# Adaptive-weight units moved from two expert layers' value stages to three feed-forward layers, and gate groups spread over the late expert units

## The reference

```python
def peer_ffn(h, w_q, sub_keys, u, v):          # first block, both layers
    q = (xc @ w_q); s = einsum(q, sub_keys)    # scores against 2 x 128 keys per head
    ... top 16 of each half, top 16 of the 256 sums -> eid, g = softmax(cv)
    a = gelu(einsum('td,thkd->thk', xc, u[eid]))
    return einsum('thk,thkd->td', g * a, v[eid])

def second_block(...):
    c_act = silu(c)
    for l in range(2):
        mod = c_act @ ada_w[l] + ada_b[l]      # 9 vectors
        h = rmsnorm(x, ...) * (1 + sc1) + sh1; y = swiglu(h, ...)        # ffn
        x = x + 0.5 * g1 * rmsnorm(y, ...)
        h = ...; y = hybrid_mixer(h, ...)                                # attention
        h = ...; y = swiglu(h, ...)                                      # ffn
```

## Time and profile before

| | |
|---|---|
| median of 3 runs | 3534.74 us |
| runs | 3529.9 to 3535.18 us |
| profiled execution | 3530.44 us |
| its span (first to last instruction) | 3528.7 us |
| TensorE busy | 3265.3 us, 93% of the span |
| VectorE busy | 2171.8 us, 62% |
| ScalarE busy | 1543.9 us, 44% |
| GpSimd busy | 469.3 us, 13% |
| mean granted TensorE clock | 0.950 |
| moved by DMA | 632.32 MB, mean 179 GB/s |

### The profile page before, as it was taken

How to read it: one execution, slowest core, us unless ns; L and a number is a source line. 1 busy time by engine, 2 the same in 40 slices (tenths; PEclk the granted TensorE clock), 3 DMA queues, 4 the chain that set the end, 5 groups by cost and what they waited for, 6 DMA issues and landing times.

```text
span 3528.7 us, 60815 instructions
## 1 busy us (share of the span) xinstructions
PE 3265.3 (93%) x20336; PEld 2856.0 (81%) x20336; DVE 2171.8 (62%) x4110; ACT 1543.9 (44%) x2941; POOL 469.3 (13%) x563
## 2 busy tenths in 40 slices
PE   6999999899998889999999999989896998988898
PEld 4779999877776745789998777779875998986798
DVE  6538878778884144288787788865433545534354
ACT  2123478744442133234788444454322444433343
POOL 0120035611110000100356111100000000000000
PEclk9999999999999766999999999999998999999899
DMA  7664544389994300345443898855431553543354
GB/s 277 219 203 157 172 156 136 115 322 317 313 313 144 107 30 18 131 159 172 158 136 109 312 317 311 312 182 184 148 133 60 184 183 127 184 134 104 102 184 143
DMA packets 176451, 632.32 MB, mean 179 GB/s; under 512 B 23608, under 2 KB 23616, under 8 KB 175328
## 3 DMA queue, kind: packets, MB, share of 16 engines
q1 hardware_dynamic: 134416, 491.48, 40.9%
q0 software_dynamic: 41920, 139.60, 11.4%
q10 hardware_dynamic: 16, 0.01, 0.0%
HBM read 627.74 MB, written 9.50 MB: 181 GB/s over the span
## 4 chain that ended last, share of the span: by engine, by line
PE 86%; DVE 7%; ACT 2%; DVEq 2%; issue 1%; POOL 1%; DMA 1%; ACTq 0%; SPq 0%; POOLq 0%
PE ps L531 20%; PE ps L411 15%; PE ps L421 10%; PE ps L423 10%; PE ps L422 10%; PE ps L519 2%; PE ps L517 2%; PE ps L518 2%; PE ps L433 2%; PE ps L464 2%; PE ps L442 2%; PE ps L788 1%; PE ps L789 1%; PE ps L494 1%; DVE unit_low L1203 1%
## 5 line engine op out<-in xcount | busy, mean ns | idle before, releaser
L1203 DVE TENSOR_TENSOR unit_low<-ring,unit_high 128x1024 fp32r<-128x1024 f32 x744 | 948.6, 1275 | 446.9 <-ACT unit_high L868 436.4
L868 ACT CAST unit_high<-ring 128x1024 fp32r<-128x1024 f32 x744 | 778.1, 1046 | 678.6 <-PE ps L423 522.6
L421 PE MATMUL ps<-expert_x_high,unit_high 128*128 128x256 f32 x1792 | 517.1, 289 | 17.6 <-DVE unit_low L1203 17.4
L422 PE MATMUL ps<-expert_x_low,unit_high 128*128 128x256 f32 x1792 | 505.0, 282 | 0.0
L423 PE MATMUL ps<-expert_x_high,unit_low 128*128 128x256 f32 x1792 | 503.6, 281 | 0.0
L411 PE MATMUL ps<-hT,ring 128*128 128x256 f32 (+1 forms) x1776 | 414.6, 393 | 49.9 <-ACT hT L903 27.2
L411 PEld LDWEIGHTS ps<-hT,ring 128*128 128x128 f32 (+1 forms) x1776 | 341.7, 195 | 114.6 <-issue 49.2
L421 PE MATMUL ps<-norm_parts,unit_high 128*128 128x256 f32 x1408 | 403.2, 286 | 27.4 <-DVE norm_parts L1208 27.4
L423 PE MATMUL ps<-norm_parts,unit_low 128*128 128x256 f32 x1408 | 401.5, 285 | 0.0
L422 PE MATMUL ps<-norm_parts,unit_high 128*128 128x256 f32 x1408 | 400.5, 284 | 0.0
L421 PEld LDWEIGHTS ps<-expert_x_high,unit_high 128*128 128x128 f32 x1792 | 342.6, 191 | 25.6 <-DVE unit_low L1203 12.4
(11 more groups left out here) (219 smaller groups left out, 5210.1 us busy)
## 6 DMA issues: line engine op xcount, KB each, us to landing
ring<-stream SPq DMA_DIRECT2D x914, 512.0 KB, 3.3
score<-ada POOLq DMA_DIRECT2D x224, 512.0 KB, 5.2
arena<-bias_tiles POOLq DMA_DIRECT2D x48, 192.0 KB, 2.7
arena<-ada SPq DMA_DIRECT2D x8, 1024.0 KB, 17.2
bias_tiles<-bias_rows POOLq DMA_DIRECT2D x8, 768.0 KB, 16.7
x_home<-x POOLq DMA_DIRECT2D x2, 1024.0 KB, 4.1
hT<-cond POOLq DMA_DIRECT2D x2, 1024.0 KB, 6.0
x<-x_home POOLq DMA_DIRECT2D x2, 1024.0 KB, 7.9
```

The lines of the kernel that those rows point to most:

```text
L421: pe.matmul(out, hi[:, kt, :], xh[:, kt, :], start=(kt == 0), stop=False)
L422: pe.matmul(out, hi[:, kt, :], xl[:, kt, :], start=False, stop=False)
L868: nc.scalar.copy(hi, ring[:, unit % SLOTS, :]).then_inc(whi_ready, 1)
L1203: V.tensor_tensor(out=lo, in0=ring[:, unit % SLOTS, :], in1=hi, op=ALU.subtract).then_inc(wlo_ready, 1)
```

## The change

- In each value stage 48 adaptive units are computed instead of 96, in two of five units from unit 10 on; the code is written out, without a loop. `cond_late` holds one condition row of 1024 instead of two.
- The other 96 are computed in ffn0, ffn1 and ffn2, 32 in each: one with each of 16 of the 22 pairs and one with each of 16 of the down units. They have slots and a condition row of their own in `arena` (`ada_ffn`, `cond_ffn`); GpSimd issues their transfers, ScalarE the silu at the start of ffn0. VectorE's loops there are written out.
- The late expert units are handled as 2 x 28 with 32 gate groups in each 28: the units 6, 13, 20 and 27 of each 28 carry two groups, the others one. TensorE loops twice over 28 units, ScalarE and VectorE are written out.

```diff
-SINGLE = 48
+LOOP_UNITS = 28
+LOOP_GATES = 32
+ADA_FFN = EARLY + 96
+        def gates_after(e):
+            return range(LOOP_GATES * e // LOOP_UNITS, LOOP_GATES * (e + 1) // LOOP_UNITS)
...
-                with pe.Fori(0, SINGLE // 4) as i:
-                    for e in range(4):
-                        expert(DIRECT + BEFORE + e, i, 4)
-                        gate(e, i, 4)
-                for e in range(NE - DIRECT - BEFORE - SINGLE):
-                    expert(DIRECT + BEFORE + SINGLE + e)
-                    gate(SINGLE + 2 * e)
-                    gate(SINGLE + 2 * e + 1)
+                with pe.Fori(0, 2) as i:
+                    for e in range(LOOP_UNITS):
+                        expert(DIRECT + BEFORE + e, i, LOOP_UNITS)
+                        for g in gates_after(e):
+                            gate(g, i, LOOP_GATES)
...
             def ffn(ph, no, u):                      # ScalarE
+                if no == 0:
+                    act.wait_ge(c_late_in, 16 * 3)
+                    nc.scalar.activation(cond_ffn, cond_ffn, ACT.Silu).then_inc(c_ready, 1)
...
+            def ada_next(n, cond_row):               # VectorE
+                v, k = n // KD, n % KD
+                ada_unit(v % 3, k, n, cond_row)
+                if k == KD - 1:
+                    ada_take(v, v % 3)
...
+                for f in range(NF):                  # feed-forward, pairs
...
+                    V.tensor_tensor(out=hparts[:, 1, f, :], in0=hid[:, e, :], in1=hparts[:, 0, f, :],
+                                    op=ALU.subtract).then_inc(hlo_ready, 1)
+                    if no < 3 and 4 <= f < 20:
+                        if no == 0 and f == 4:
+                            dve.wait_ge(c_ready, 4)
+                        ada_next(m, cond_ffn)
+                        m += 1
+                for f in range(NF - 2):              # down units
+                    low(u + f + 2, n + f + 2)
+                    if no < 3 and f < 16:
+                        ada_next(m, cond_ffn)
+                        m += 1
...
+                def weigh_loop(it, last):
+                    for e in range(LOOP_UNITS):
+                        for g in gates_after(e):
+                            weigh(g, it, LOOP_GATES)
+                            if g == gates_after(e)[0]:
+                                low(u + DIRECT + BEFORE + e + 2, n + DIRECT + BEFORE + e + 2, it, LOOP_UNITS)
+                            if not last or g + 2 < LOOP_GATES:
+                                columns_hot(g + 2, it, LOOP_GATES)
                         dve.drain()
-                        unit_times(DIRECT + BEFORE + e, i, 4)
+                        unit_times(DIRECT + BEFORE + e, it, LOOP_UNITS)
                         dve.drain()
...
-                        if 6 <= e < 30 if late else e % 4 < 3:      # in turn(), 96 in a stage
+                for e in range(NE):
+                    if e + 2 < NE:
+                        activations_low(e + 2, a + e + 2)
+                        low(u + e + 2, n + e + 2)
+                    if e >= 8 and e % 5 in (0, 2):
+                        if m == EARLY + 48 * l:
+                            dve.wait_ge(c_ready, 2 + l)
+                        ada_next(m, cond_late)
+                        m += 1
...
-                pool.dma_start(cond_late, cond.to_broadcast([P, 2 * D])).then_inc(c_late_in, 16)
+                pool.dma_start(cond_late, cond[0:1, l * D:(l + 1) * D].to_broadcast([P, D])).then_inc(c_late_in, 16)
...
+            def ffn(ph, no):                         # GpSimd
+                if no == 0:
+                    pool.wait_ge(x_ready, KD * phases.index(ph))
+                    pool.dma_start(cond_ffn, cond[0:1, D:2 * D].to_broadcast([P, D])).then_inc(c_late_in, 16)
+                m = ADA_FFN + 32 * no
+                for q in range(m, m + 32):
+                    if q >= ADA_FFN + SLOTS:
+                        pool.wait_ge(ada_used, q - SLOTS + 1)
+                    pool.dma_start(ada_ffn[:, q % SLOTS], ada[q]).then_inc(ada_late[q % SLOTS], 16)
```

More of the change, by code:

```diff
@@ L1114, in rows_hot @@
                     for t in range(4):
-                        nc.scalar.activation(hot[:, g % 2, 2, t, :], iota, ACT.Square, bias=oT4[:, 0, it + g // 4, g % 4, t:t + 1])
+                        nc.scalar.activation(hot[:, g % 2, 2, t, :], iota, ACT.Square, bias=oT4[:, 0, it * (per // GB) + g // GB, g % GB, t:t + 1])
                     act.drain()
@@ L1133, in peer, with rows_loop @@
                         rows_hot(1)
-                with act.Fori(0, SINGLE // 4) as i:
-                    for e in range(4):
-                        gelu_aside(DIRECT + BEFORE + e, i, 4)
-                        rows_hot(e + 2, i, 4)
-                for e in range(NE - DIRECT - BEFORE - SINGLE):
-                    gelu_aside(DIRECT + BEFORE + SINGLE + e)
-                    for g in range(SINGLE + 2 * e + 2, min(SINGLE + 2 * e + 4, S // 4)):
-                        rows_hot(g)
+                def rows_loop(it, last):
+                    for e in range(LOOP_UNITS):
+                        gelu_aside(DIRECT + BEFORE + e, it, LOOP_UNITS)
+                        for g in gates_after(e):
+                            if not last or g + 2 < LOOP_GATES:
+                                rows_hot(g + 2, it, LOOP_GATES)
+                rows_loop(0, False)
+                rows_loop(1, True)
                 u += NE
@@ L1307, in take_outputs, with ada_unit @@
                 V.tensor_copy(oT[HD:P, chunk, :], ps[bank + 1][HD:P, 0:S]).then_inc(o_read, 1)
-            def ada_unit(c, k, n, cond_row, it=0, per=0):
+            def ada_unit(c, k, n, cond_row):
                 if n < FIRST:
@@ L1669, in peer @@
                 dve.drain()
-                with dve.Fori(0, SINGLE // 4) as i:
-                    for e in range(4):
-                        weigh(e, i, 4)
-                        low(u + DIRECT + BEFORE + e + 2, n + DIRECT + BEFORE + e + 2, i, 4)
-                        columns_hot(e + 2, i, 4)
+                def weigh_loop(it, last):
+                    for e in range(LOOP_UNITS):
+                        for g in gates_after(e):
+                            weigh(g, it, LOOP_GATES)
+                            if g == gates_after(e)[0]:
+                                low(u + DIRECT + BEFORE + e + 2, n + DIRECT + BEFORE + e + 2, it, LOOP_UNITS)
+                            if not last or g + 2 < LOOP_GATES:
+                                columns_hot(g + 2, it, LOOP_GATES)
                         dve.drain()
-                        unit_times(DIRECT + BEFORE + e, i, 4)
+                        unit_times(DIRECT + BEFORE + e, it, LOOP_UNITS)
                         dve.drain()
-                for e in range(NE - DIRECT - BEFORE - SINGLE):
-                    for g in range(SINGLE + 2 * e, SINGLE + 2 * e + 2):
-                        weigh(g)
-                        if g + 2 < S // 4:
-                            columns_hot(g + 2)
-                        if g % 2 == 0:
-                            low(u + DIRECT + BEFORE + SINGLE + e + 2, n + DIRECT + BEFORE + SINGLE + e + 2)
-                    dve.drain()
-                    unit_times(DIRECT + BEFORE + SINGLE + e)
-                    dve.drain()
+                weigh_loop(0, False)
+                weigh_loop(1, True)
                 u += NE
@@ L1696, in activations_low @@
                                     op=ALU.subtract).then_inc(alo_ready, 1)
[L1698 to L1714 removed]
                 for k in range(2):
                     activations_low(k, a + k)
[L1718 to L1725 removed]
+                m = EARLY + 48 * l
+                for e in range(NE):
[7 more added lines that the diff above has]
+                        m += 1
+                assert m == EARLY + 48 * (l + 1)
                 wait_used(dve, u + NE - 1)
@@ L1878, in _ @@
                     hyb(ph, int(ph[-1]))
+                elif ph != "ffn3":
+                    ffn(ph, int(ph[-1]))
 def vec_of(ph):
```

82 lines of the change are left out of this document (25 added, 57 removed).

## The result

| | us, median | runs | profiled execution | its span |
|---|---|---|---|---|
| before (same chip) | 3532.59 | 8 | 3530.44 (run ahead of the change) | 3528.7 |
| changed | 3559.99 | 8 (3546.1 to 3571.98) | 3557.78 | 3555.3 |

Ratio 1.0077, 95% interval 1.0056 to 1.0098: 27 us slower. The forecast was 3545.5 with a range of 3518 to 3568, so the direction and the range held, and the size was short by 14 (as a difference: +10.8 forecast, +27.4 measured). Beside this the changed kernel scatters by 26 us between executions, the kernel before by 8.

What follows compares the result with a forecast made beforehand. The chain of waits, 86% of it TensorE's, was taken as the bound. Terms -1.3 - 2.3 + 0.5 + 6.4 + 7.5 = +10.8 gave 3541 for the profiled execution, 3545.5 as a median; range 3518 to 3568.

Steps and rivals of the forecast that it cites:

- part 3: Late expert units: spreading the gate groups makes each double wait 2.3, +3.2 a stage, +6.4 for both, clock apart.
- Part 1: Value stages: 48 adaptive units fewer in each save nothing themselves; shorter silu -1.3, hardware loop gone -2.3.
- the steady state: Value stages: units hang on TensorE, ScalarE's cast and VectorE's low part, so removing adaptive units gains 0.
- -1.3: Start of both value stages: the shorter silu removes TensorE's idle of 0.64 behind it, twice; bounds 0 and -2.6.
- -2.3: Second value stage: removing VectorE's hardware loop takes its length from 379.9 towards the first's 377.6; bounds 0 and -2.3.
- a rule that would have given up to 81 a stage: Value stages: queues share 16 DMA engines, so 48 transfers fewer could save up to 81 us; forecast took 0.
- Part 2: ffn0 to ffn2: 96 adaptive units fit VectorE's gaps under ScalarE's cast; +0.5 for all three layers, bounds 0 and +14.
- adaptive units lengthen the layers: Feed-forward layers: only 0.2 of room in each gap, +14 on top, 3559; chance 0.06.
- 1.6 that is always there, and 0.7 by which VectorE has fallen behind: First double of the late expert units: the two pieces of TensorE's forecast wait of 2.3 for its second gate.
- 5 x 0.16: Later doubles: VectorE falls behind 0.16 a unit after each double, raising their wait from 1.6 up to 2.4.
- the third rival: Late expert units: VectorE's unit drops to 3.7 or less, waits 1.6, no clock fall; -8, 3527; chance 0.22.
- TensorE's clock: Doubles of the late expert units: three falls to half clock at 2.5 each among 16 waits, +7.5.

Runs made afterwards that it cites:

- ada_moved_alone: Changed kernel with the gate groups put back behind single units and the last eight doubled, so only the adaptive units are moved: 3549.95 us, ratio 1.0055.
- no_late_units: Changed kernel without any adaptive unit's transfer or product in the value stages and feed-forward layers: 3547.4 us, ratio 1.0049.
- gates_spread_alone: Kernel before with only the gate groups spread; adaptive units stay in the value stages: 3551.7 us, ratio 1.0063.
- columns_first: Changed kernel with VectorE's column one-hots issued ahead of the weight low part in every late unit: 3534.4 us, ratio 1.0010.
- before_columns_first: Kernel before with column one-hots ahead of the low part in the 48 single late units and VectorE's second value-stage loop written out: 3511.1 us, ratio 0.9948.
- no_jump: Changed kernel with TensorE's loop of two passes of 28 late units written out: 3552.4 us, ratio 1.0068.

## Why the prediction was right in sign and short in size

**Where it fell short.** In the spans it is 26.6 against 10.8. Of the 15.8 between them, 7.1 lie in hyb0 and hyb1 and 2.8 in stages that nothing here touched, both forecast as 0; 5.1 in the late units, 1.8 in the feed-forward layers, and the value stages gave 0.9 more than forecast. That the total came no further out is in part luck: in part 3 a wait that was put too long stood against a clock and a jump that were put too low.

**Part 1, value stages: the steady state right, the size by luck.** Forecast -1.3 and -2.3; measured -4.5 together in this profile, -3.1 in ada_moved_alone. The steady state was put at 0 against a rule that would have given up to 81 a stage, and no_late_units shows 0. The Trainium skill (Trainium Kernel Development and Optimization, section Key Constraints) is right that the queues share 16 engines; what decides is whether anything waits. The -1.3 came for another reason than forecast. The silu is shorter, 1.06, but TensorE still idles 0.56 behind it in the changed kernel, where it idled 0.64:

```profile
733.64 1.06 ACT L1166 ACTIVATE hT<-hT 128x1024 f32<-128x1024 f32 x1
737.25 0.50 PE L539 MATMUL ps<-unit_high,expert_high 128*128 128x512 f32 x1 [0.56 <-DVE unit_low L1212]
```

What went are idles of 0.69 (peer0, 720.99) and 1.27 (peer1, 1960.77) ahead of the silu, behind casts that waited for the ring. In peer1 the idle behind the silu is new. Before:

```profile
718.63 1.05 ACT L868 CAST unit_high<-ring 128x1024 fp32r<-128x1024 f32 x1 [0.68 <-DMA ring<-stream]
1958.41 1.05 ACT L868 CAST unit_high<-ring 128x1024 fp32r<-128x1024 f32 x1 [1.25 <-DMA ring<-stream]
```

That is -0.8 and -0.7; the forecast had such transfers only in its bound of -2.6. The loop written out gave 1.2 to 1.5, not 2.3. Some 1.3 to 1.6 of peer1's -3.5 is then in neither and stays open (with the stage unedited, gates_spread_alone has 396.0 where the kernel before has 395.1, so about 1 can be scatter); peer1's stage as a whole is 1.9 to 3.6 shorter in the ten kernels with the moved units, peer0's between 1.2 shorter and 0.4 longer.

**Part 2, feed-forward: the failed term.** I costed it at +0.5 by VectorE's room, in the gate-and-up part. There it was right: with those units alone the layers take 586.6. I never costed its transfers. The down part's 24 products were read as VectorE's roomiest place, and they are the tightest for the DMA engines: one adaptive unit for each unit of the ring. Measured: +1 to +8 by execution, most of it in the down parts, and 0.7 to 1.7 in ffn1's gate-and-up part. With either half left out that second wait is gone too; why it stands there is not shown. The rival "adaptive units lengthen the layers" had the sign, with +14, by the wrong mechanism.

**Part 3, spread gates: short by 5 for both stages, made of wrong pieces.** Forecast 2 x 3.2 and 7.5 for the clock, 13.9; measured 19.0. I had 5.13 from weigh to gate and a wait of 2.3; measured 5.37 and 1.7. The step that failed is "1.6 that is always there, and 0.7 by which VectorE has fallen behind". The 5.13 was read where the low part on the way took 1.70 instead of 1.22:

```profile
658.13 1.70 DVE L1203 TENSOR_TENSOR unit_low<-ring,unit_high 128x1024 fp32r<-128x1024 f32 x1
```

So 0.48 of it is not always there. It is VectorE's delay too, in another place. Without the collision the way is 5.13 - 0.48 = 4.65 there and 5.37 - 0.71 = 4.66 here. In the changed kernel TensorE is free 3.69 behind weigh (at 498.59; 498.11, as I took it, in the kernel before, whose stage started 0.32 earlier). That leaves 0.97 that is always there, and 0.71 of delay: 1.68. For the doubles behind the first I put 5 x 0.16 on top of the 1.6 and so counted 0.48 twice; for the first I took the delay over as it stood in the kernel before, 0.7 at weigh and 0.48 in the low part at once.

The delay per unit is as forecast, only that up to a double it no longer shows at weigh. In the changed kernel weigh comes every 3.72, at TensorE's pace, but the low part grows from unit to unit, by 0.14, and the column one-hots behind it stand 3.86 apart, as in the kernel before:

```profile
480.63 1.36 DVE L1212 TENSOR_TENSOR unit_low<-ring,unit_high 128x1024 fp32r<-128x1024 f32 x1
481.91 0.67 DVE L1670 TENSOR_TENSOR column_hots<-prm,ps 128x512 f32<-128x512 f32 x1
484.35 1.50 DVE L1212 TENSOR_TENSOR unit_low<-ring,unit_high 128x1024 fp32r<-128x1024 f32 x1
485.77 0.67 DVE L1670 TENSOR_TENSOR column_hots<-prm,ps 128x512 f32<-128x512 f32 x1
...
499.25 2.05 DVE L1212 TENSOR_TENSOR unit_low<-ring,unit_high 128x1024 fp32r<-128x1024 f32 x1
501.22 0.67 DVE L1670 TENSOR_TENSOR column_hots<-prm,ps 128x512 f32<-128x512 f32 x1
```

The 3.86 are made by both engines in a ring: column one-hots at 497.36, GpSimd's two products from 498.18 to 500.23, the low part, held up by them, to 501.30, and the next column one-hots at 501.22. With the one-hots first they stand 3.72 apart, in columns_first and in before_columns_first. In gates_spread_alone the low part reached 2.05 before the first double in both stages, weigh then came late as well, and that double waited 2.05 and 2.00.

By my own mark ("waits under 2.0") the third rival should have come about: VectorE keeps up, 3527, with no fall of the clock. The mark was met and the rival was not: weigh keeps up, the one-hots don't, and the clock fell. The mark could not tell a shorter unit from a shorter delay.

In the forecast's own frame, from weigh 0 to the weigh of gate 62, peer0 took 235.8 against 229.9. Five falls x 1.35 = 6.7, and 3.5 for the jump, are 10.2 of it. The 225.6 that are left are 4.3 under the forecast, mostly by its waits of 2.4 that were 1.7, and 1.1 under the 226.7 of the kernel before, whose first double has a fall in it as well (0.62 over the 4 us from 662.66).

**TensorE's clock: mis-sized, and its reason false.** Forecast 3 falls at 2.5 because a wait of 2.3 lies between 1.54 (no fall) and 2.64 (fall). Measured: waits of 1.68 to 1.76 with falls at 12 of 16, 8 of the 12 that stand alone, and 1.35 a fall. The scale of lengths that the earlier trace rows seemed to give is no scale: 1.54 held the clock and 2.91 held it, and 1.68 didn't. Waits of 0.69 had no fall in all the doubles that stand alone. Ten falls lie between the doubles of the two stages, about +13. They are no independent trials either. In no_jump, where no jump comes between, the clock over the 4 us behind peer0's eight doubles read 1.00, 0.58, 0.62, 0.67, 0.71, 1.00, 0.57, 0.58: a row of falls, each a little less deep in that stretch, then one double passed over, then the same again. Why is not shown.

**The jump: not in the forecast.** 3.5 and 3.1 by the changed kernel's spacings, -3.6 and -2.3 when removed, 5.5 and 5.4 with the columns first. I weighed what loops cost on VectorE, where one was taken away, and not on TensorE, where one of 4 units was replaced by one of 28.

**hyb0 and hyb1: not settled.** Each is 0.9 to 3.8 longer where it is not 116.4. In the traces those are the ones in which TensorE's clock falls a second time at the start of the stage. It is longer in 9 of 12 cases with all the adaptive transfers in the layer ahead, in 3 of 4 with half of them, and in 3 of 12 with none or an eighth of the bytes. So it is more frequent with them and not bound to them. What separates the 28 cases of the table without exception is the moment of the clock's first fall, in the idle time ahead of the stage. In the 13 cases at 116.4 it starts 11.9 to 12.2 ahead of the stage's first query product; in the other 15 it starts earlier (12.3 to 14.8) or later (11.5 to 11.8), and a second fall follows. So the 7.1 may be no more than a shift of that moment, which any edit ahead of it can bring. Why the second fall comes is not shown.

## What to carry to other kernels

Spreading a stall evenly makes as many chances for the clock to fall as there are stalls; shorten its cause first, here by one swap on VectorE that puts the producer that others wait for ahead of the one that nobody waits for yet, and that leaves the delay of their collision to the engine with more time to spare. Before a delay is added to a length read from a trace, the rows within that length should be searched for it. When work moves to another stage, divide its bytes by that stage's unit time, part by part, as well as looking for engine room. When a hardware loop's body grows, look for idle time that ends in "issue" at its jump.

## What the hardware showed that I had not expected

- TensorE's jump back over a body of 28 units (928 matmuls) took 2.3 to 4.0 us of idle with no releaser; over 4 units (128 matmuls), none above 0.15.
- A wait of TensorE of 1.68 in otherwise gapless work was followed by half clock in two cases of three, at 1.35 us a time (once 2.8); one of 0.69 never.
- VectorE's low part and GpSimd's product delay each other one way only: 1.22 and 1.89 if VectorE starts first, 1.93 and 1.04 if GpSimd does. In the second order the pair made a unit of 3.86, in the first 3.72, TensorE's pace.
- With the ring alone a 512 KB transfer landed in 3.3 in the feed-forward layer; with the adaptive units beside it in 4.6 in the gate-and-up part, 4.9 in the down part, and over 6 where TensorE's chain had to wait for one.
